# Where a list of stages begins: ring places of raw tiles, rounded weight pieces and PSUM pairs counted per list or through the program, and a general wait

## What is computed

```
x = first_block(x, meta_tokens, ...)      # 2 layers, L = 16 meta tokens + 256
    h = layer_norm(concat(meta, x))
    per layer: u = h @ w_in
               mix = (sigmoid(ga) * attention(q, k, v) @ w_attn_proj
                      + sigmoid(gc) * conformer_conv(glu) @ w_conv_proj) @ w_out
               h = layer_norm(ALPHA * h + mix)
               f = swiglu(h)  (layer 0)   or   moe_swiglu(h), 8 experts, top 2  (layer 1)
               h = layer_norm(ALPHA * h + f)
return second_block(x, c, ctx, ...)       # 2 layers, 256 latent + 256 context tokens
    per layer: ffn_sublayer, attention (neighborhood / sliding-window GQA), ffn_sublayer,
               each with modulation by c and layer_norm(ALPHA * h + gate * y)
```

## Time and profile before

| | |
|---|---|
| median of 3 runs | 3487.79 us |
| lowest, highest | 3481.81, 3491.05 us |
| profiled execution, its own time | 3495.14 us |
| its span, first to last instruction | 3493.4 us |
| mean granted TensorE clock (1 is full) | 0.952 |
| busy: TensorE, VectorE, ScalarE, GpSimd | 93%, 58%, 45%, 16% |

### The profile page before, as it was taken

One profiled execution on the slowest core, in us unless ns is written; L12 is line 12 of the kernel. 1 busy time (PEld: TensorE's weight loads), 2 busy tenths in 40 slices (PEclk: granted clock), 3 DMA queues, 4 the chain that ended last, 5 costly groups with the idle time before them and its releaser, 6 DMA issues.

```text
span 3493.4 us, 64859 instructions
## 1 busy us (share of the span) xinstructions
PE 3257.5 (93%) x26454; PEld 3073.7 (88%) x26454; DVE 2014.5 (58%) x3240; ACT 1562.7 (45%) x2670; POOL 568.5 (16%) x671
## 2 busy tenths in 40 slices
PE   7779998779999999999999998999999999988898
PEld 7669998569999999999999996789999999965798
DVE  6855559454555555667457645584466636765555
ACT  4335443344444444455335445453354424544544
POOL 3500008400000000113001412160012300130000
PEclk9779999589999999999999999999999999988999
DMA  5313544336788877555345440243454435440253
GB/s 221 128 49 134 183 146 156 96 125 237 291 300 296 293 285 276 197 197 202 115 154 191 175 163 27 73 150 129 150 188 170 161 109 182 147 167 1 85 197 105
DMA packets 106058, 580.68 MB, mean 166 GB/s; under 512 B 17105, under 2 KB 29521, under 8 KB 52858
## 3 DMA queue, kind: packets, MB, share of 16 engines
q1 hardware_dynamic: 89376, 489.54, 39.7%
q0 software_dynamic: 13568, 84.91, 7.0%
q10 hardware_dynamic: 2842, 2.34, 0.2%
HBM read 575.08 MB, written 11.04 MB: 168 GB/s over the span
## 4 chain that ended last, share of the span: by engine, by line
PE 82%; DVE 9%; ACT 4%; issue 2%; POOL 1%; DMA 1%; ACTq 0%; SPq 0%; DVEq 0%; POOLq 0%
PE PS L1003 70%; PE PS L1166 4%; DVE CONV L1846 3%; DVE WL L1605 3%; PE PS L1145 2%; PE PS L1040 2%; PE PS L1155 1%; POOL TMP L910 1%; ACT WH L1296 1%; PE PS L1120 1%; PE PS L1185 0%; ACT PT L1457 0%; DVE RSTD L1622 0%; PE PS L1124 0%; DVE TMP L1701 0%
## 5 line engine op out<-in xcount | busy, mean ns | idle before, releaser
L1605 DVE TENSOR_TENSOR WL<-RAW,WH 128x1024 fp32r<-128x1024 f32 (+1 forms) x1018 | 1164.9, 1147 | 929.1 <-ACT WH L1296 922.4
L1003 PE MATMUL PS<-UH,WH 128*128 128x256 f32 (+1 forms) x5536 | 1537.7, 284 | 87.9 <-DVE WL L1605 23.6
L1003 PE MATMUL PS<-UL,WH 128*128 128x256 f32 (+1 forms) x5536 | 1525.3, 282 | 0.0
L1003 PE MATMUL PS<-UH,WL 128*128 128x256 f32 (+1 forms) x5536 | 1525.2, 282 | 0.0
L1296 ACT ACTIVATE WH<-RAW 128x1024 fp32r<-128x1024 f32 (+1 forms) x1018 | 985.1, 969 | 1035.5 <-PE PS L1003 1009.8
L1003 PEld LDWEIGHTS PS<-UH,WH 128*128 128x128 f32 x5536 | 1044.0, 191 | 115.4 <-issue 99.6
L1003 PEld LDWEIGHTS PS<-UH,WL 128*128 128x128 f32 x5536 | 1043.2, 191 | 0.0
L1003 PEld LDWEIGHTS PS<-UL,WH 128*128 128x128 f32 x5536 | 1042.6, 191 | 0.5
L1003 PE MATMUL PS<-HIDH,WH 128*128 128x256 f32 (+1 forms) x2112 | 547.8, 280 | 0.0
L1003 PE MATMUL PS<-HIDH,WL 128*128 128x256 f32 (+1 forms) x2112 | 544.6, 278 | 0.0
L1003 PE MATMUL PS<-HIDL,WH 128*128 128x256 f32 (+1 forms) x2112 | 544.4, 278 | 0.0
(11 more groups left out here) (186 smaller groups left out, 2546.2 us busy)
## 6 DMA issues: line engine op xcount, KB each, us to landing
RAW<-in_w_gu SPq DMA_DIRECT2D x255, 1024.0 KB, 4.9
RAW<-in_w_dn SPq DMA_DIRECT2D x168, 704.0 KB, 4.1
MRAW<-in_w_mod POOLq DMA_DIRECT2D x36, 1024.0 KB, 6.2
TMP<-in_w_mod POOLq DMA_DIRECT2D x36, 1024.0 KB, 7.2
RAW<-in_w_in SPq DMA_DIRECT2D x30, 1024.0 KB, 6.2
RAW<-in_w_na SPq DMA_DIRECT2D x20, 1024.0 KB, 4.9
RAW<-in_w_o SPq DMA_DIRECT2D x12, 1024.0 KB, 4.9
RAW<-in_w_proj SPq DMA_DIRECT2D x8, 1024.0 KB, 4.9
```

Of the source, the lines that this page charges most:

```text
L1003: last = pe.matmul(ps[:, a:b], w, m[:, a:b], start=first and a == 0, stop=final and b == n)
L1605: dve.tensor_tensor(WL[slot][:, 0:hi - lo], RAW[:, s % RAW_SLOTS, lo:hi], WH[slot][:, 0:hi - lo].bitcast(F32), ALU.subtract).then_inc(s_lo, 1)
```

## The change

`Phase` gets `first`, the number of its first step in the whole program. RAW place, piece places and PSUM pair are all worked out from `first + s`. The user before is then always the step 4 places back (RAW, PSUM) or the piece 4 back, in whichever list it lies. `begin` waits from the program's fifth step on. `in_steps` no longer calls `all_evacuated`; `straight` and proj still do. The arguments for loops over iterations (`n_iter`, `i`), which were 1 and 0 everywhere, go; proj keeps its own choice of PSUM banks. The diff to its core; the calls follow the new signatures:

```diff
-    def __init__(self, name, prev, n_iter, kinds, cols, last, steps=None):
-        ...
-            self.p0 = prev.p0 + prev.pieces * prev.n_iter
-            self.raw0 = [prev.raw0[r] + prev.n_iter * len(range(r, prev.n, RAW_SLOTS)) for r in range(RAW_SLOTS)]
+    def __init__(self, name, prev, kinds, cols, steps=None):
+        self.name, self.prev, self.next, self.kinds, self.cols, self.steps = name, prev, None, kinds, cols, steps
+        self.n = len(kinds)
+        self.first = self.a0 = self.d0 = 0
         if prev is not None:
             prev.next = self
+            self.first, self.a0, self.d0 = prev.first + prev.n, prev.evacs("a"), prev.evacs("d")
+        self.p0 = self.piece(0, 0)
+
+    def piece(self, s, h):
+
+        return PIECES * (self.first + s) + h
 
     def piece_slot(self, s, h):
-        return (PIECES * s + h) % PIECE_SLOTS
+        return self.piece(s, h) % PIECE_SLOTS
+
+    def raw(self, s):
+        return (self.first + s) % RAW_SLOTS
+
+    def bank(self, s):
+        return 2 * ((self.first + s) % BANK_SETS)
...
-    def raw_user(self, i, s):
-
-        if s >= RAW_SLOTS:
-            return self.piece(i, s - RAW_SLOTS, PIECES - 1) + 1
-        return self.piece(i, 0, 0) - PIECES * self.behind(s % RAW_SLOTS)
+    def raw_user(self, s):
+
+        return self.piece(s - RAW_SLOTS, PIECES - 1) + 1
+
+    def piece_user(self, s, h):
+
+        return self.piece(s, h) - PIECE_SLOTS + 1
+
+    def bank_user(self, s):
+
+        p, s = self, s - BANK_SETS
+        while s < 0:
+            p = p.prev
+            s += p.n
+        return p.kinds[s], p.evacs(p.kinds[s], s + 1)
...
-                if not (p.prev is None and s < RAW_SLOTS):
-                    sp.wait_ge(s_lo, p.raw_user(i, s))
-                sp.dma_start(RAW[:, s % RAW_SLOTS, 0:p.cols[s]], src).then_inc(s_raw[s % RAW_SLOTS], 16)
+                if p.first + s >= RAW_SLOTS:
+                    sp.wait_ge(s_lo, p.raw_user(s))
+                sp.dma_start(RAW[:, p.raw(s), 0:p.cols[s]], src).then_inc(s_raw[p.raw(s)], 16)
...
-                if s >= BANK_SETS:
-                    kind, count = p.bank_user(i, s)
+                if p.first + s >= BANK_SETS:
+                    kind, count = p.bank_user(s)
                     pe.wait_ge(s_evd if kind == "d" else s_eva, count)
...
                 p = ph[name]
-                all_evacuated(p)
                 seen = []
```

More of the change, by code:

```diff
@@ L156, in evacs @@
[L156 to L171, removed]
@@ new lines, in step_ahead @@
+    def step_ahead(self, s):
+        if s + AHEAD < self.n:
+            return self, s + AHEAD
+        return self.next and (self.next, s + AHEAD - self.n)
+    def raw_user(self, s):
[8 more added lines that the diff above has]
+        return p.kinds[s], p.evacs(p.kinds[s], s + 1)
@@ L542, in ups @@
         def ups(n):
-            p = ph[n]
-            return sum(t == "u" for t, _, _, _ in p.steps) if p.steps else KH * p.n_iter
+            return sum(t == "u" for t, _, _, _ in ph[n].steps)
         SIL_BASE, base = {}, 0
@@ L767, in _ @@
                         if s >= RAW_SLOTS:
-                            load(ph["wo0"], 0, s, ins["w_o"][0][k])
+                            load(ph["wo0"], s, ins["w_o"][0][k])
                     in_steps("fb0", 2 + N_EXP + 2)
@@ L1286, in _, with high, ahead @@
             act.dma_start(SK2[:, :], ins["sinks_2"].to_broadcast([P, 16])).then_inc(s_const, 16)
-            def high(p, i, s, h):
+            def high(p, s, h):
                 if h == 0:
-                    act.wait_ge(s_raw[s % RAW_SLOTS], p.loads(i, s) * 16)
+                    act.wait_ge(s_raw[p.raw(s)], p.loads(s) * 16)
                 lo, hi = bounds(p, s, h)
                 slot = p.piece_slot(s, h)
-                if not (p.prev is None and s < 2):
-                    act.wait_ge(s_pc, p.piece_user(i, s, h))
-                act.activation(WH[slot][:, 0:hi - lo], RAW[:, s % RAW_SLOTS, lo:hi], ACT.Copy).then_inc(s_hi, 1)
-            def ahead(p, i, s, pieces=range(PIECES)):
-                later = p.step_ahead(i, s)
+                if p.piece(s, h) >= PIECE_SLOTS:
+                    act.wait_ge(s_pc, p.piece_user(s, h))
+                act.activation(WH[slot][:, 0:hi - lo], RAW[:, p.raw(s), lo:hi], ACT.Copy).then_inc(s_hi, 1)
+            def ahead(p, s, pieces=range(PIECES)):
+                later = p.step_ahead(s)
                 for h in pieces if later else ():
@@ L1503, in _ @@
                 for h in range(PIECES):
-                    high(ph["win0"], 0, s, h)
+                    high(ph["win0"], s, h)
             act.wait_ge(s_vec, 16)
@@ L1567, in _ @@
             for s in range(4):
-                ahead(ph["wo1"], 0, s)
+                ahead(ph["wo1"], s)
             norm("2n1", H, H, V_B + 48 + 16, NMETA, SEQ, u=modulated_u("fb1", NMETA, SEQ))
@@ L1598, in __exit__, with low, ahead @@
                         own.n = self.n0 + self.per * self.n_iter
-            def low(p, i, s, h):
+            def low(p, s, h):
                 lo, hi = bounds(p, s, h)
                 slot = p.piece_slot(s, h)
-                dve.wait_ge(s_hi, p.piece(i, s, h) + 1)
-                dve.tensor_tensor(WL[slot][:, 0:hi - lo], RAW[:, s % RAW_SLOTS, lo:hi],
+                dve.wait_ge(s_hi, p.piece(s, h) + 1)
+                dve.tensor_tensor(WL[slot][:, 0:hi - lo], RAW[:, p.raw(s), lo:hi],
                                   WH[slot][:, 0:hi - lo].bitcast(F32), ALU.subtract).then_inc(s_lo, 1)
-            def ahead(p, i, s, pieces=range(PIECES)):
-                later = p.step_ahead(i, s)
+            def ahead(p, s, pieces=range(PIECES)):
+                later = p.step_ahead(s)
                 for h in pieces if later else ():
@@ L1852, in _ @@
                 for h in range(PIECES):
-                    low(ph["win0"], 0, s, h)
+                    low(ph["win0"], s, h)
             norm("emb", H, 0, L1, low_u("win0", 0, L1))
```

218 lines of the change are left out of this document (102 added, 116 removed).

## The result

The changed kernel takes 3456.69 us, median of four runs (3451.76 to 3462.93), against 3484.80 of the kernel before, median of four (3481.57 to 3491.05). The ratio is 0.9929, with a 95% interval of 0.9906 to 0.9951. It was timed twice more, on two other occasions and chips (1 and 9): 0.9920 (0.9891 to 0.9948) and 0.9903 (0.9865 to 0.9940). The mean of the three ratios, 0.9917, is 28.8 us of 3485; the forecast was 31.3 us, which taken from the earlier median of three, 3487.79, gave 3456.5.

What follows compares the result with a forecast made beforehand. TensorE, busy for 93% of the span, was taken to bound the kernel, with its waits and lost clock to win. Terms 25.64 + 1.61 + 4.08 = 31.3 us, from the 3487.79 median, gave 3456.5 us (chance 0.77); range 3447 to 3469.

Steps and rivals of the forecast that it cites:

- The three boundaries: Fa0 to naqkv, fb0 to fa1, fa1 to waqkv: idle time and slow step 0 go, 8.99 + 8.60 + 8.05 = 25.64 us.
- rival B: The clock falls anyway, owed to the length of work, so only idle time is won: 23.3 us, 3464.5 us; chance 0.08.
- moe to fa0: All places match already before fa0, so only the general wait for evacuations goes: 1.61 us.
- win0 and win1: VectorE's idle times before WL pieces of proj's step 0 go, so attention starts earlier: 2.70 + 1.38 = 4.08 us.
- Rival C: In win0 and win1 the gain is eaten, other engines' work setting attention's start: 27.3 us, 3460.5 us; chance 0.06.
- wo0 to fb0: At fb0's start the evacuation wait moves behind UL's first chunk, both idle times together staying 4.59 us: nothing won.
- the bound of 3.1: At fb0's start, upper bound in us if the 42 matmuls after the wait run at full clock; taken as nothing.
- rival D: A new wait at the mean matmul replaces the removed one at three places: 5.7 us left, 3482.1 us; chance 0.04.
- Rival E: The change doesn't do what it says; some other order keeps the first tile late: about 3482 us; chance 0.03.
- rival F: Slower: TensorE, now without rests, is held at its low clock more often: loss over 10.5 us, 3498 us; chance 0.02.
- The PSUM pairs are not what costs there: At the 65-step lists' ends, the general wait asks for every evacuation, whichever pair comes next; no size given.

Runs made afterwards that it cites:

- the later variance: The changed kernel with the variance of the eight-step half norms taken one step later; against the kernel before 0.9870, the second time 0.9899 beside the changed kernel's 0.9903.

## Why the prediction was right, and where it was not

**The three boundaries** were forecast at 8.99, 8.60 and 8.05 us. Taken as above (14.47, 14.06 and 13.53 less 5.45) they gave 9.02, 8.61 and 8.08. Of the 25.7 us 17.56 were idle time; the rest is step 0 at a low clock, and three times the 0.16 of overlap. That the low clock was owed to the stop and not to the unbroken work before it (rival B, 3464.5) is shown: after some 360 us without a rest longer than 1.4, the ends of fa0, fb0 and fa1 run at 1.00 in every profile of the changed kernel. The Trainium skill, "TensorE: Matmul & The Clock Gate", section "What's actually happening", has activity releasing the clock, and these traces agree with it: 1.00 in the unbroken stretches.

**moe to fa0** was forecast at 1.61 and gave 1.86 us: 7.31 less 5.45. The quarter of a microsecond more is the overlap and a step 0 that takes 5.61 us without a stop and 5.70 behind one.

**win0 and win1** were forecast at 2.70 + 1.38. From the last product of win0 to the first of proj it was 81.84 us and is 79.07, 2.8 less. For win1 it was 79.39 and is 77.36, 2.0 less, but the second profile of the changed kernel shows 79.63 there and the first with the later variance 79.67, so only the first holds in all. Where the 2.0 came, the stretch from wout1's last product to moe's first was shorter too, 38.74 us for 40.05; no term had this, and why it moves is open. A wider measure is the end of moe's last product in the eleven profiles. In the four kernels that count pieces per list it is 1592.8 to 1595.7 us, in six of the seven profiles with pieces counted through the program 1587.1 to 1589.7; the seventh (1595.7) has slower products in the last 170 us of moe. The term was 4.08, is 4.8 by the two places and 5.8 by these means without the seventh, 4.8 with it. The step that placed it was too simple in one point: TensorE's wait for the exponentials hardly shrank (4.81 to 4.64 us); what shrank was its wait ahead of the first transposes of attention's values (2.66 to 0.78), so the wait that the prediction named is not the one that gave. Rival C, a gain eaten there, did not come true.

**wo0 to fb0** was forecast at nothing, with one wait of about 4.8 us in place of two. The wait is 4.66 us. But the 42 products behind it are faster than the 7.91 us of the earlier trace rows, as the chain shows:

```profile
2300.10 7.24 PE PS L980 x42
```

So 0.7 us came out of the bound of 3.1 that the text had kept for the range.

**No new wait** (rival D). At naqkv GpSimd's last addition ended at 1966.69, 3.1 us after naqkv's first product began, and the mean matmul is due 5.6 us after that beginning: hidden by 2.5 us, where the forecast had 2.3 at fa0. GpSimd's timeline:

```profile
1964.93 1.76 POOL L880 TENSOR_TENSOR TMP<-TMP,H 128x256 f32<-128x256 f32 x1 [1.97 <-DVE H L1690]
```

**Rival E** fell with the issue of the first tile at 1947.19, **rival F** with the clock of 1.00.

**The step that failed** is a sentence of the explanation, not a term: "The PSUM pairs are not what costs there". The stop was a chain of two halves in series: the late tile and pieces, and behind them the evacuations that TensorE asks for. Moving the pairs and dropping the wait cuts the chain after the first piece (17.6 of 25.7 us at the three boundaries), and moving RAW and pieces makes the evacuations early (20.8). Either gives most of the gain and the second adds the rest. What gives nothing is the wait made exact with the pairs left where they were (1.0004), and little comes from half of the tile and piece places (0.9977 and 0.9985). The prediction took the pairs and their wait as one part, the tile and piece places as another, and gave the cost to the second, so it could not see this; its total did not depend on it, since the change moves everything at once.

**The sum.** By its own terms the two profiles differ by 9.02 + 8.61 + 8.08 + 1.86 + 4.8 + 0.7 = 33.1 us, and their spans by 32.2. That the two are close is luck: two larger differences, neither owed to the change, nearly cancel. One is the interval between products told in the last section. Fa0's 65 steps took 374.4 us in place of 364.4 by it, fa1's 366.1 in place of 377.5 (2.6 of these 11.4 are step 0 at the low clock, counted above), fb1 was slower and part of fb0 faster. Added up from moe on, as what each interval of 112 to 120 ns has over 113.3, it cost the changed kernel 26.0 us and the kernel before 20.4. The other is the last attention, from waqkv's last product to wo1's first: 128.63 us in place of 135.22. The changed kernel's own second profile has 135.17 there, and the granted clock goes with it (columns as in the earlier trace rows; before, the changed kernel, its second profile):

```profile
3119.70:3254.90 135.20, 106.94 (x493) 70.62 (x492) 74.07 (x231) 54.09 (x142) 6.33 (x16) 0.82 0.03 11
3085.00:3213.60 128.60, 99.93 (x492) 64.84 (x492) 74.17 (x231) 54.15 (x142) 6.37 (x16) 0.88 0.04 13
3085.40:3220.50 135.10, 106.41 (x492) 69.71 (x492) 74.28 (x231) 54.19 (x142) 6.33 (x16) 0.83 0.03 13
```

Without both the spans would differ by 32.2 + 5.6 - 6.6 = 31.2 us. That the median came within 0.2 us of the forecast 3456.5 is luck as well: the medians differ by 28.1 us and not by 31.3, and the kernel before measured 3.0 us less than the median that the forecast started from.

## What to carry to other kernels

Where a pipeline's buffers start again at place 0 in each stage, count what the last step of one stage and the first of the next share, for every ring; in a ring of four steps a stage of 4n + 1 steps leaves the least room, in a ring of two (the rounded pieces here) any odd number does. One counter through the program removes this, and no cost of it shows in the traces. An exact wait is worth nothing while the place it guards was used last a moment ago. When two causes lie in one chain, removing each by itself says how much it can give and never how much of the total is its own: here two parts gave 6.1 and 0.4 us apart and 20.8 together, and a third 17.6 without them, of the same 25.7.

## What the hardware showed besides

In unbroken work at a granted clock of 1.00, products of 256 columns follow each other at one of two intervals, 113.3 or 117.8 ns. The same 200 us of fa0 (1640 to 1840), products at the line of piece_product only, hold 1701 of them in the first profile of the changed kernel (columns: length, busy time and count of PE and PEld, clock, DMA share, GB/s):

```profile
1640.00:1840.00 200.00, 200.00 (x1701) 200.00 (x1700) 1.00 0.40 137
2400.00:2500.00 100.00, 100.00 (x885) 100.00 (x884) 1.00 0.32 111
```

and 1767 in the second one, which is slow in 2400 to 2500 instead:

```profile
1640.00:1840.00 200.00, 200.00 (x1767) 200.00 (x1767) 1.00 0.41 142
2400.00:2500.00 100.00, 100.00 (x851) 100.00 (x851) 1.00 0.35 121
```

The third (span 3437.9 us, the shortest of all) has 1767, 884 and 885 in the windows 1640, 2400 and 2780. Same program, same clock, DMA load much alike: the placement of the kernel does not decide it alone. It may have a share, for the first 640 us of moe ran at the short interval in all eleven profiles.

An interval lasts for tens to hundreds of us. Counted from moe on in the eleven profiles, it became long 62 times, and 56 of these lie across an idle time of TensorE. It became short 58 times, and 30 of these lie across the two mean matmuls, with no idle time at all. Five changes to the long one have neither, and one stands behind the 16 small products at 1430.74 in the second profile. So a stop is not needed for a change, as the second possibility of the expectation for the later variance had it. In its second profile the chain goes from 117.6 to 113.7 ns a product there:

```profile
1868.00 6.00 PE PS L980 x51
1874.00 0.43 PE PS L1049 x2
1874.43 7.62 PE PS L980 x67
```

One slow stretch of 270 us costs 270 x (1 - 113.3/117.8) = 10 us. The profiles have two to six slow stretches of some 20 to 270 us each from moe on. By the sum used above they cost from 5.9 us (the third profile of the changed kernel) to 35.9 (the general wait alone replaced). The first and the third profile of the changed kernel differ in it by 20.1 us, and in their spans by 23.3. Together with the 8 us of the last attention this is the size of the scatter between runs of one kernel, so effects under some 10 us have to be read from the boundaries in the trace. The Trainium skill, "TensorE: Matmul & The Clock Gate", section "Wait — 56ns, not 53.3ns?", gives N / 2.4 GHz + 2.5 ns for warm back-to-back products of N columns. By this figure of the page 109.2 ns is the estimate for 256 columns, and neither level meets it. What sets the level stays open.

The granted clock bore short rests: over the 14 us around each it was 1.00 at idle times of 1.2 and 1.6 us, 0.88 at 2.08 us, and 0.76 at 6.03 us. The length does not settle it alone: the three stops of 4.51 us of the kernel with RAW places only gave 0.76, 0.88 and 0.88.

GpSimd's additions for a half norm (the line of the earlier trace rows) have two lengths, too. In the trace of the kernel before, the 30 that begin just before a WL subtraction of VectorE take 0.73 to 0.75 us. The 20 that begin while one is running end 0.58 to 0.60 us after it ends, and take 1.25 to 1.77 us in all.
